# The candidate steps of ScalarE's top-k searches done by POOL in two-scalar operations, with 18 rounds on ScalarE and 8 on VectorE

## What is computed

```
score = einsum('bqh,bqhk->bqk', wi, relu(einsum('bqhd,bkd->bqhk', qi, ki))) * INDEX_SCALE
score = where(vis, score, -inf)            # key's chunk of 64 not after the query's
_, sel = top_k(score, 256)
logits = (q @ k[sel]) * ATTN_SCALE + bias[bucket(sel - qpos)]
o = softmax(logits) @ v[sel]
y = x + rmsnorm(concat(pooled * silu(gate_a), o * silu(gate_b)) @ w_out)
```

## Time and profile before

| | us |
|---|---|
| median of 3 runs | 1619.12 (1618.85 to 1619.71) |
| profiled execution, its own time | 1615.77 |
| its span | 1614.0 |
| TensorE busy in the span | 1497.7 (93%) |
| VectorE busy | 1139.6 (71%) |
| ScalarE busy | 894.3 (55%) |
| POOL busy | 461.1 (29%) |

### The profile page before, as it was taken

One profiled execution on the slowest core, in us unless ns is written; L12 is line 12 of the kernel. 1 busy time (PEld: TensorE's weight loads), 2 busy tenths in 40 slices (PEclk: granted clock), 3 DMA queues, 4 the chain that ended last, 5 costly groups with the idle time before them and its releaser, 6 DMA issues.

```text
span 1614.0 us, 17120 instructions
## 1 busy us (share of the span) xinstructions
PE 1497.7 (93%) x4935; PEld 842.8 (52%) x4935; DVE 1139.6 (71%) x2742; ACT 894.3 (55%) x1684; POOL 461.1 (29%) x387
## 2 busy tenths in 40 slices
PE   7999899989999999988888999898998989999997
PEld 4555555555554787756444444444444444455552
DVE  5412577869999655765478999999999889874412
ACT  3112333333343545552798999888997877533331
POOL 0111211121111322311434555344423233232341
PEclk9999999999999999989799999999999999999999
DMA  9322222231111211136813332331130211103111
GB/s 369 70 61 49 74 54 64 56 103 47 64 50 43 66 47 42 50 91 191 256 38 90 87 93 61 94 100 61 43 106 27 70 39 46 66 20 110 34 33 52
DMA packets 93159, 125.69 MB, mean 78 GB/s; under 512 B 17310, under 2 KB 64222, under 8 KB 92683
## 3 DMA queue, kind: packets, MB, share of 16 engines
q1 hardware_dynamic: 91834, 120.68, 24.1%
q10 hardware_dynamic: 1232, 3.93, 2.2%
HBM read 75.93 MB, written 47.61 MB: 77 GB/s over the span
## 4 chain that ended last, share of the span: by engine, by line
PE 26%; DVE 17%; issue 7%; ACT 3%; POOL 0%; POOLq 0%; DVEq 0%; ACTq 0%
PE wide L1792 8%; PE wide L1777 8%; DVE above L345 6%; DVE max_junk L1853 4%; PE bank L1752 2%; PE bank L1753 2%; PE bank L1754 2%; PE bank L1725 2%; ACT act_junk L1667 1%; DVE above L377 1%; DVE root L296 1%; DVE reach L378 1%; PE wide L1725 1%; DVE search L349 1%; DVE root L299 1%
## 5 line engine op out<-in xcount | busy, mean ns | idle before, releaser
L938 PE MATMUL bank<-hT,home 128*128 128x512 f32 (+2 forms) x1280 | 486.0, 516 | 5.1 <-DVE sga L1153 2.4
L1627 POOL TENSOR_TENSOR E<-E,home 128x512 f32<-128x512 f32 (+1 forms) x174 | 231.9, 1337 | 448.3 <-ACT E L1705 448.1
L938 PEld LDWEIGHTS bank<-hT,home 128*128 128x128 f32 x1280 | 235.0, 191 | 165.0 <-issue 142.9
L1777 PE MATMUL wide<-E,home 128*128 128x512 f32 x544 | 284.1, 604 | 0.8 <-POOL E L1627 0.7
L1705 ACT ACTIVATE E<-bank 128x512 f32<-128x512 f32 (+1 forms) x290 | 165.1, 569 | 196.7 <-PE bank L1754 178.8
L914 ACT ACTIVATE relu<-wide 128x1024 f32<-128x1024 f32 (+7 forms) x192 | 154.1, 803 | 210.8 <-PE wide L956 159.7
L1192 DVE SCALAR_TENSOR_TENSOR S<-relu,wi,S 128x1024 f32<-128x1024 f32 (+7 forms) x168 | 173.8, 1034 | 102.2 <-ACT relu L914 95.0
L1853 DVE CUSTOM_DVE_ANT_0 max_junk<-bank,mask 128x512 bf16<-128x512 f32 (+3 forms) x235 | 138.3, 607 | 84.3 <-PE bank L1725 72.6
L1667 ACT ACTIVATE act_junk<-S,minus_cand 128x1152 uint8<-128x1152 f32 (+5 forms) x105 | 155.4, 1480 | 1.6
L1792 PE MATMUL wide<-home 128*128 128x512 f32 x272 | 140.9, 609 | 14.2 <-ACT osb L1690 14.1
L956 PE MATMUL wide<-kiT,qiT 96*128 96x512 f32 (+3 forms) x304 | 139.4, 528 | 5.8 <-ACT relu L914 5.8
(11 more groups left out here) (215 smaller groups left out, 2194.5 us busy)
## 6 DMA issues: line engine op xcount, KB each, us to landing
xs<-x_prompt SPq DMA_DIRECT2D x16, 512.0 KB, 4.3
home<-w_in SPq DMA_DIRECT2D x16, 512.0 KB, 13.0
xr<-x_prompt SPq DMA_DIRECT2D x16, 512.0 KB, 4.1
y_prompt<-osb SPq DMA_DIRECT2D x16, 512.0 KB, 2.8
first_q<-q_high_scratch SPq DMA_DIRECT2D x24, 256.0 KB, 4.8
s_scratch<-S SPq DMA_DIRECT2D x11, 512.0 KB, 2.7
gb<-gb_scratch SPq DMA_DIRECT2D x17, 256.0 KB, 5.0
home<-ma_scratch SPq DMA_DIRECT2D x17, 256.0 KB, 5.0
```

The lines of the kernel that those rows point to most:

```text
L938: mm = pe.matmul(out, stationary(c), moving(c), start=(c == 0), stop=(c == DC - 1))
L1627: pool.tensor_tensor(E[:, k % 4, :, 0:n], E[:, k % 4, :, 0:n], EB[:, kv * GRP:(kv + 1) * GRP, off:off + n], ALU.mult)\
L1777: pe.matmul(wide[0][:, kv * 512:kv * 512 + GRP * n].rearrange("p (j n) -> p j n", j=GRP), values[:, kt, kv:kv + 2, :].rearrange("p a d -> ...
```

## The change

`ZOOM_AT` goes from 16 to 18, in the first phase's searches too, where it only moves the shift of scores by two rounds. T leaves ScalarE. POOL does it in two operations: `act_side = (act_sum >= limit) * (-2 half_width)` with two constants, and `minus_cand = act_side + minus_cand + half_width`, with a column and a constant (in the first round only the constant). The column `enough` and its 11 memsets go. The semaphore `halved` is split into `counted` (ScalarE) and `moved` (POOL). A count now waits for POOL's second operation, POOL's first for ScalarE's count, VectorE's continuation for POOL's last. In the orders N stands at a, the 18 counts from a + 0.3 to b, and POOL's pair of round r 0.35 of a gap behind its count.

```diff
--- before.py
+++ after.py
@@ -61,7 +61,7 @@
 
 
 LEAST = -3e38
-ZOOM_AT = 16
+ZOOM_AT = 18
 ALL_ROUNDS = 26
 ROUND_TRIP = 14.0
 EXPONENT = 0x7F800000
@@ -1272,7 +1272,12 @@
 
     NSK = PAST // P + 1
     FIRST = EARLY[-1] + 1
-    HALVED = 1 + 3 * ZOOM_AT
+
+    def counted_by(t, r):
+        return (1 + ZOOM_AT) * (t - FIRST) + 1 + r
+
+    def moved_by(t, r):
+        return 2 * (ZOOM_AT * (t - FIRST) + r)
 
     def searched(t):
 
@@ -1359,10 +1364,8 @@
             if t == ST:
                 series.append(([("Z",)], start[t + 1], 0.0))
         for u, (a, b, _) in bounds.items():
-            pieces = [("N", u)]
-            for r in range(ZOOM_AT):
-                pieces += [("K", u, r), ("T", u, r)]
-            series.append((pieces, a, b))
+            series.append(([("N", u)], a, a))
+            series.append(([("K", u, r) for r in range(ZOOM_AT)], a + 0.3, b))
         return in_order(series)
 
     def pool_order():
@@ -1372,6 +1375,9 @@
                        ([("A", t - 1)] if 0 <= t - 1 < NT else [], when(t, 0.33), 0.0),
                        ([("P", t - 3)] if 0 <= t - 3 < NT else [], when(t, 0.67), 0.0)]
         series.append(([("V",)], bounds[ST - 2][2] + 2.0, 0.0))
+        for u, (a, b, _) in bounds.items():
+            gap = (b - a - 0.3) / ZOOM_AT
+            series.append(([("T", u, r) for r in range(ZOOM_AT)], a + 0.3 + 0.35 * gap, b + 0.35 * gap))
         return in_order(series)
 
     def sp_order():
@@ -1414,7 +1420,6 @@
         act_junk = sb(st, "act_junk", [P, SEQ], U8)
         act_sum, act_side = (sb(st, f"act_search{i}", [P, 1], F32) for i in range(2))
         minus_cand = sb(st, "minus_cand", [P, 2], F32)
-        enough = sb(st, "enough", [P, NT], F32)
         junk = sb(st, "max_junk", [P, 2, 512], BF16)
         qh = [first_q[0], first_q[1], sb(st, "qh2", [P, NKV, GRP, P], F32R)]
         ql = [first_q[2], sb(st, "ql1", [P, NKV, GRP, P], F32R)]
@@ -1451,8 +1456,7 @@
         xr_in = sem("xr_in")
         y_out = [sem(f"y_out{i}") for i in range(2)]
         dk = sem("dk")
-        enough_set = sem("enough_set")
-        halved, cand_taken = sem("halved"), sem("cand_taken")
+        counted, moved, cand_taken = sem("counted"), sem("moved"), sem("cand_taken")
         mask_ready, mask_out = sem("mask_ready"), sem("mask_out")
         plain_mask = sem("plain_mask")
         fx_full, fx_free = sem("fx_full"), sem("fx_free")
@@ -1606,14 +1610,25 @@
                                      onesb[HD:P, :].rearrange("p (a n) -> p a n", a=1).broadcast_to([P - HD, NPT, P]))                        .then_inc(k2u_ones, 1)
                 pool.wait_ge(k2u_ones, 1 + NKV)
                 pool.memset(vx[:, :, 1, :], 2.0).then_inc(vx_set, 1)
-                for t in range(FIRST, NT):
-                    pool.memset(enough[:, t:t + 1], key_tiles(t) * P - 2.0 * TOPK + 1.5).then_inc(enough_set, 1)
                 pool.wait_ge(eb_in, 16)
                 for kind, *at in pool_order():
                     if kind == "A":
                         mean(at[0])
                     elif kind == "P":
                         residual(at[0])
+                    elif kind == "T":
+                        u, r = at
+                        if r == 0 and u >= FIRST + 2:
+                            pool.wait_ge(cand_taken, u - FIRST - 1)
+                        pool.wait_ge(counted, counted_by(u, r + 1))
+                        pool.tensor_scalar(act_side[:], act_sum[:], 2.0 * TOPK - 1.5 - key_tiles(u) * P, -2.0 * half_width(r),
+                                           ALU.is_ge, ALU.mult).then_inc(moved, 1)
+                        pool.wait_ge(moved, moved_by(u, r) + 1)
+                        mc = minus_cand[:, u % 2:u % 2 + 1]
+                        if r == 0:
+                            pool.tensor_scalar(mc, act_side[:], half_width(r), None, ALU.add).then_inc(moved, 1)
+                        else:
+                            pool.tensor_scalar(mc, act_side[:], mc, half_width(r), ALU.add, ALU.add).then_inc(moved, 1)
                     elif kind == "V":
 
                         pool.wait_ge(mask_ready, ST - 2 - FIRST + 1)
@@ -1645,42 +1660,27 @@
 
                 load_q_tile(act, ql[1][:].bitcast(F32), q_dram[1], 1, ql_in[1], 1)
 
-                def halved_by(t, r, part):
-                    return HALVED * (t - FIRST) + 1 + 3 * r + part
-
-                act.wait_ge(enough_set, NT - FIRST)
                 waiting = []
                 for kind, *at in act_order():
                     if kind == "N":
                         u = at[0]
                         s = S[sslot(u)][:, 0:key_tiles(u) * P]
                         act.wait_ge(S_in[sslot(u)], 16 * ((u - FIRST) // 3 + 1))
-                        act.activation(s, s, ACT.Copy, scale=unit[:, u:u + 1]).then_inc(halved, 1)
+                        act.activation(s, s, ACT.Copy, scale=unit[:, u:u + 1]).then_inc(counted, 1)
                     elif kind == "K":
                         u, r = at
                         w = key_tiles(u) * P
-                        act.wait_ge(halved, halved_by(u, r, 0))
+                        if r == 0:
+                            act.wait_ge(counted, counted_by(u, 0))
+                        if moved_by(u, r):
+                            act.wait_ge(moved, moved_by(u, r))
                         if r == 0:
                             act.activation(act_junk[:, 0:w], S[sslot(u)][:, 0:w], ACT.Sign, accum_out=act_sum[:])\
-                               .then_inc(halved, 1)
+                               .then_inc(counted, 1)
                         else:
                             act.activation(act_junk[:, 0:w], S[sslot(u)][:, 0:w], ACT.Sign,
                                            bias=minus_cand[:, u % 2:u % 2 + 1], accum_out=act_sum[:])\
-                               .then_inc(halved, 1)
-                    elif kind == "T":
-                        u, r = at
-                        if r == 0 and u >= FIRST + 2:
-                            act.wait_ge(cand_taken, u - FIRST - 1)
-                        act.wait_ge(halved, halved_by(u, r, 1))
-                        act.activation(act_side[:], act_sum[:], ACT.Sign, bias=enough[:, u:u + 1])\
-                           .then_inc(halved, 1)
-                        act.wait_ge(halved, halved_by(u, r, 2))
-                        mc = minus_cand[:, u % 2:u % 2 + 1]
-                        if r == 0:
-                            act.activation(mc, act_side[:], ACT.Copy, scale=-half_width(r)).then_inc(halved, 1)
-                        else:
-                            act.activation(mc, act_side[:], ACT.Identity, scale=-half_width(r), bias=mc)\
-                               .then_inc(halved, 1)
+                               .then_inc(counted, 1)
                     elif kind == "Y":
                         b, i = at
                         act.wait_ge(o_full, 2 * b + i + 1)
@@ -1823,7 +1823,7 @@
                 def continue_search(u):
 
                     nonlocal n
-                    dve.wait_ge(halved, HALVED * (u - FIRST + 1))
+                    dve.wait_ge(moved, moved_by(u, ZOOM_AT))
                     dve.tensor_scalar(B.cand[:], minus_cand[:, u % 2:u % 2 + 1], -1.0, None, ALU.mult)\
                        .then_inc(cand_taken, 1)
                     dve.wait_ge(cand_taken, u - FIRST + 1)
```

## The result

The changed kernel takes 1708.24 us in the median of 4 runs (1705.19 to 1710.38), the kernel before beside it 1618.98 (4 runs): a ratio of 1.0547, 95% interval 1.0529 to 1.0565. It is 89 us slower; the forecast was 54 slower.

A forecast was written before the change was run, and what follows sets the result against it. ScalarE was taken to have no room up to 1008 us, VectorE to be late after 1187. ScalarE 46, unfilled room 10, VectorE -7 and collisions 5 gave +54 us, hence 1673 us; range 1624 to 1728.

The forecast's parts named there:

- The rival behind that part: Much slower: POOL's pair takes 0.89 us and often waits for VectorE's scan or product; 1731 us, chance 0.10 over 1705.
- The pair: POOL's two dependent operations after each count take 0.59 us, with ends at 0.37 and 0.89.
- What bounds the kernel, and the order of the cases: Second phase: ScalarE has no room up to 1008 us, VectorE is late after 1187; gaps behind a product cost most.
- The rival that saw VectorE as the bound: Faster: POOL answers in ScalarE's shadow and VectorE's late rounds come back whole; 1605 us, chance 0.12.
- The price of a gap: ScalarE idle between two counts: 0.83 us with nothing between, 0.35 with an exponential, 2.12 with its product ahead on POOL.
- a gap behind a product: Between two counts, an exponential's bias product stands ahead of the pair on POOL: 2.12 us idle on ScalarE.
- the four lists in the prediction: ScalarE's waits for POOL: 37.3 us in tiles 6 and 7, 54.9 in 8 to 10, 43.3 in 11 to 13, 41.6 after.
- unfilled room: Up to tile 13, a third of ScalarE's 30.3 us of waits for TensorE stays unfilled: +10 us.
- collisions: One POOL pair in ten of the first 8 tiles' 144 loses 0.4 us to VectorE's operations: +5 us.
- The room: ScalarE's waits for TensorE absorb its losses: 8.9 us in tiles 6 and 7, 4.7, 16.7, then 43.4 in 14 to 16.
- VectorE's relief: From 1187 us on, six fewer VectorE rounds of at most 2.34 us gain 0 to 14 us; half taken, -7.
- The first phase, "no time": In the early tiles' searches only the shift of scores moves, by two rounds: no time.

The follow-up runs named there:

- pair_next: The changed kernel with POOL's pair placed 0.02 instead of 0.35 of a gap behind its count: 1660.47 us, ratio 1.026.
- noscan_before: The kernel before without VectorE's scan and the sum behind it in tiles 6 to 16: 1598.77 us, ratio 0.9868.
- act18: The kernel before with 18 rounds on ScalarE and 8 on VectorE, no POOL in the search: 1636.86 us, ratio 1.0115.
- pair_next16: The changed kernel with POOL's pair 0.02 of a gap behind its count and 16 rounds on ScalarE: 1625.18 us, ratio 1.0043.
- mixed16: The kernel before with POOL's steps, right behind the count, only in tiles 11 to 16, still 16 rounds on ScalarE: 1611.92 us, ratio 0.9962.
- noscan_after: The changed kernel without VectorE's scan and the sum behind it in tiles 6 to 16: 1683.08 us, ratio 1.0388.
- idle_pairs: The kernel before with POOL also doing two one-column operations on spare columns after every ScalarE count, nobody waiting: 1614.5 us, ratio 0.9978.

## Why the prediction was right in kind and 35 us short

1708 us lies in the stated range, but in the part over 1705 us that had a chance of 0.10. The rival behind that part had a slow pair that is often shut out. The pair wasn't slow; that it is often shut out came true.

**What bounds the kernel, and the order of the cases: right.** Up to 1008 us ScalarE had no room, and there the time was lost; the stretches after tile 13 kept their length. TensorE's waits moved from VectorE to ScalarE. The rival that saw VectorE as the bound needed the exponentials behind the count to have waited anyway; they hadn't, as the 1.98 us at 982.31 and pair_next's 48 us show. It was right in that VectorE's work was on the path before (noscan_before, 19 us), but act18, which relieves VectorE at ScalarE's cost, loses 19 us.

**The pair: right.** Forecast 0.22 + 0.17 + 0.20 = 0.59 us, measured in the clean case 0.23 + 0.10 + 0.30 = 0.63, from 983.85 to 984.48. The operation with a column as operand was never under 0.302 us.

**The price of a gap: right.** The profile counts idle time from the end of ScalarE's last instruction, while the prices count from where the next could have started, which is 0.10 us earlier (a count at 987.59 starts 0.10 before the exponential of 987.11 to 987.69 ends). With these 0.10 us a gap behind a product took 2.08 where 2.12 was forecast, a covered one 0.36 where 0.35 was, and a bare one 0.84 (0.74 idle before the count at 978.39) where 0.83 was. All the waits of ScalarE for POOL come to 166 us in 128 gaps, 179 with the 0.10; the sum of the four lists in the prediction was 177. By stretch (us):

| tiles | waits for POOL, forecast | measured | growth, forecast | measured |
|---|---|---|---|---|
| ahead of 6 | - | - | 0 | 8.5 |
| 6, 7 | 37.3 | 32.1 | 12.4 | 18.6 |
| 8 to 10 | 54.9 | 58.2 | 27.8 | 45.1 |
| 11 to 13 | 43.3 | 49.4 | 6.1 | 20.8 |
| 14 to 16, to the end | 41.6 | 26.2 | 0, less 7 for VectorE | 1.5 |

(15 us of the forecast, unfilled room and collisions, had no place. The measured waits are the profile's; with 0.10 us for each they are 34.7, 62.3, 52.9 and 28.8.) The measured growths add to that of the span, 94.4 us; the forecast for it was 54.

**The room: the step that failed.** I let ScalarE's waits for TensorE shrink by what it lost to POOL. In tiles 6 to 10 they didn't shrink at all: 19.7 and 4.7 us became 21.5 and 5.9, and 4.0 for the sums (L1656) came on top. In tiles 11 to 13 they did, 16.7 to 2.2, and the stretch grew by 20.8 all the same. The term for unfilled room, +10, was put as a third of 30.3 us and was too small. Over all five stretches the sum let 52 us of waits for TensorE be filled and took 10 back, so 42; measured, they fell by 22 us at the exponentials (84.5 to 62.7) and rose by 5 at the sums (3.0 to 7.8), so 17. These 25 us are the largest part of the 40 by which the span's growth was missed; the start of the second phase (8.5) and VectorE's relief (7) are nearly all the rest. A wait of ScalarE for POOL delays TensorE too (68.3 us behind output copies, 23.0 behind bias products), and TensorE then delays the next logits. The two engines take turns to wait, while the sum treated TensorE as a source that is always ahead. The amounts are measured; that this mutual delay is the reason for them is read from the waits and wasn't tested by a run of its own.

**TensorE's own pace: not in the sum.** In tiles 8 to 10 it does 386 matmuls in 144.27 us, where the earlier trace rows has 388 in 129.82. The granted clock is 0.87, before it was 1.00; full is 2.4 GHz, so part of the stretch was at the lower of its two levels, 1.2 GHz. Before that TensorE was 91% busy in this stretch, and now it is 77%. With 8 us in tiles 6 and 7 and 7 in 11 to 13, for as many matmuls, some 30 of the 36 us by which its busy time grew over the span lie in these three stretches. It goes with the waits: at 200 us from the same place (867 to 1067) the clock is 0.91 in pair_next, 0.95 in pair_next16 and 1.00 in mixed16. How much of these 30 us is in the 40 us of the miss wasn't separated; no run has the waits and the full clock.

**Collisions: mis-sized by a factor of eight, as durations.** Forecast were 0.4 us in one pair of ten, +5; measured are 42 us in 40 operations, so one pair in five, at 1.05 us each. What they cost in time isn't known (noscan_after and its control leave it open). Longest is this one, POOL and then VectorE:

```profile
1399.20 5.31 POOL L1631 TENSOR_SCALAR minus_cand<-act_search,minus_cand 128x1 f32<-128x1 f32 x1
```

```profile
1399.14 1.28 DVE L1908 SCALAR_TENSOR_TENSOR osb<-osb,root,gpost 128x1024 f32<-128x1024 f32 x1
1400.34 4.15 DVE L384 TENSOR_TENSOR_SCAN S<-reach,above 128x1920 f32<-128x1920 bf16 x1
```

It began 0.06 us into VectorE's product and ended with the scan behind it, at 1404.51. The prediction had the earlier trace rows for this, where one product lasts 0.93 us too long and two together 2.56, and priced 0.4. The exclusive lock that the Trainium skill describes (SBUF — State Buffer, section Who interferes with whom) is what these rows look like; it was rightly named as speaking against the change. idle_pairs shows that such a hold costs nothing until somebody waits for it. As far as the 42 us are inside the 179, and 177 were forecast without them, the clean gaps together were priced up to 40 us too high: 128 of 187 gaps show a wait, where the sum charged all. So it is in part luck that the sum of the waits came out right: two errors of about one size cancelled in it.

**VectorE's relief, -7: wrong.** The stretches after tile 13 gave back nothing net, and the split alone costs 19 us: VectorE's work was on the path, but the longer search on ScalarE takes its place.

**The first phase, "no time": probably wrong.** In the profiles the second phase starts some 4.5 us later in kernels with the shift at round 18.

## What to carry to other kernels

A short step between two long ones of a dependent chain may move to another engine only if its engine is free when it is due and something else covers the way there and back. Look at what stands ahead of it in the other queue, above all work that itself waits for the first engine: moving the pair ahead of such work was worth 40 of 48 us, and leaving out the tiles without cover turned a loss into a gain. And idle time of a waiting engine isn't safely room: 17 of the 42 us that were counted on here could be filled, and the engine waited for was itself made later by the same delay.

## What the runs showed of the hardware

- POOL: an operation on one column takes 0.22 us with constants, 0.30 with a column as second operand, and 0.10 us passes from one to a dependent one. POOL starts 0.08 us after ScalarE's sum is read out (983.77 to 983.85), ScalarE 0.03 after POOL's last (984.48 to 984.51).
- By these records a one-column operation of POOL beside a scan, a product of three operands, a sum of two bf16 tiles or a plain `tensor_scalar` over a wide row on VectorE lasts until that ends (36 of 37 that began inside one, at least 0.35 us ahead of its end), and on into the next such one if it follows at once: up to 5.31 us instead of 0.30. Beside a count with accumulation (69), a maximum (49) or a transpose (8) none was held.
- The granted clock of TensorE fell to 0.87 over 188 us in which TensorE was 77% busy, with nothing in its own program changed. A matmul there took 374 ns in the mean instead of 335.
